# A 96-byte gap in front of one weight buffer, and 32 bytes behind it

## The reference, cut to what matters

```python
u = rms_norm(h, norm1_g)
p_rwkv, p_nsa = split(u @ w_in)                  # w_in: 1024 x 3096
y = concat(rwkv7_time_mix(p_rwkv), nsa_attention(p_nsa))
h = h + y @ w_out
h = h + (silu(rms_norm(h) @ w_gate) * (rms_norm(h) @ w_up)) @ w_down      # 1024 -> 2816 -> 1024
# then, in each of two layers: half a feed-forward, a mixer (even_w_in / odd_w_in), half a feed-forward
```

## Time and profile before

| | us |
|---|---|
| median of three runs | 1424.02 |
| lowest and highest run | 1423.72 and 1424.87 |
| span of the profiled execution | 1422.4 |
| TensorE busy in it | 1395.2 |
| VectorE busy | 944.7 |
| ScalarE busy | 691.0 |

### The profile page before, as it was taken

How to read it: one execution, slowest core, us unless ns; L and a number is a source line. 1 busy time by engine, 2 the same in 40 slices (tenths; PEclk the granted TensorE clock), 3 DMA queues, 4 the chain that set the end, 5 groups by cost and what they waited for, 6 DMA issues and landing times. The chain is left out here.

```text
span 1422.4 us, 25483 instructions
## 1 busy us (share of the span) xinstructions
PE 1395.2 (98%) x10044; PEld 1286.2 (90%) x10044; DVE 944.7 (66%) x1539; ACT 691.0 (49%) x1107; POOL 82.9 (6%) x137
## 2 busy tenths in 40 slices
PE   8999999999999999999999999999999999999997
PEld 8898888999989999899989999999998988899997
DVE  5778567766668666567577666676665676676665
ACT  6764545433454443376654433444433655643342
POOL 1030010000020000000000000100000123000000
PEclk9999999999999999999999999999999999999999
DMA  9344005645526555433356545365554423465540
GB/s 359 135 160 185 2 25 228 222 177 183 197 108 228 209 184 177 178 104 133 120 207 224 189 177 182 129 229 198 194 177 178 149 90 134 177 222 180 194 158 30
DMA packets 33069, 239.47 MB, mean 168 GB/s; under 512 B 6864, under 2 KB 13280, under 8 KB 14304
## 3 DMA queue, kind: packets, MB, share of 16 engines
q1 hardware_dynamic: 30320, 234.84, 45.6%
q10 hardware_dynamic: 2672, 3.58, 0.7%
HBM read 236.15 MB, written 2.25 MB: 168 GB/s over the span
## 5 line engine op out<-in xcount | busy, mean ns | idle before, releaser
L498 PE MATMUL ps<-uT_h,w_gu 128*128 128x256 f32 x3520 | 614.1, 279 | 2.5 <-ACT uT_h L1316 2.5
L498 PEld LDWEIGHTS ps<-uT_h,w_gu 128*128 128x128 f32 x3520 | 538.0, 188 | 13.8 <-issue 5.0
L498 PE MATMUL ps<-uT_l,w_gu 128*128 128x256 f32 x1760 | 478.8, 279 | 0.0
L498 PE MATMUL ps<-w_dn,h_r 128*128 128x512 f32 x1320 | 325.7, 396 | 0.3 <-DVE h_r L2070 0.3
L498 PEld LDWEIGHTS ps<-uT_l,w_gu 128*128 128x128 f32 x1760 | 325.5, 188 | 0.0
L498 PEld LDWEIGHTS ps<-w_dn,h_r 128*128 128x128 f32 x1320 | 239.6, 188 | 51.3 <-issue 1.4
L1368 ACT CAST w_gu<-ring 128x2048 fp32r<-128x2048 f32 x110 | 210.0, 1909 | 156.2 <-PE ps L498 155.6
L2028 DVE TENSOR_TENSOR w_gu<-ring,w_gu 128x2048 fp32r<-128x2048 f32 x110 | 252.1, 2292 | 35.2 <-ACT w_gu L1368 35.2
L2061 DVE TENSOR_TENSOR us<-ps,bc 128x256 f32<-128x256 f32 x110 | 46.5, 423 | 203.2 <-PE ps L498 203.2
L1381 ACT ACTIVATE wk<-wk 128x256 f32<-128x256 f32 x110 | 46.1, 419 | 260.7 <-DVE wk L2059 260.7
L1374 ACT CAST w_dn<-ring 128x1024 fp32r<-128x1024 f32 x110 | 115.7, 1052 | 82.8 <-PE ps L498 82.7
(11 more groups left out here) (398 smaller groups left out, 1696.0 us busy)
## 6 DMA issues: line engine op xcount, KB each, us to landing
ring<-wstream SPq DMA_DIRECT2D x144, 1536.0 KB, 6.6
cst<-consts_in SPq DMA_DIRECT2D x1, 2185.0 KB, 13.7
wk<-t_row ACTq DMA_DIRECT2D x1, 2048.0 KB, 8.0
wk<-masks_in SPq DMA_DIRECT2D x1, 1216.0 KB, 24.1
x<-x_in SPq DMA_DIRECT2D x2, 512.0 KB, 4.7
ring<-wstream SPq DMA_DIRECT2D x1, 1024.0 KB, 8.8
inh<-gains ACTq DMA_DIRECT2D x2, 512.0 KB, 9.6
tri_blocks<-wk SPq DMA_DIRECT2D x3, 256.0 KB, 2.8
```

The costliest lines, as they stand in the source:

```text
L498: return pe.matmul(o, l, r, start=start, stop=stop, skip_group_check=True)
```

## The change

Two unused allocations are made: 24 floats (96 bytes per partition) ahead of inh, and 8 floats (32 bytes) behind it. inh starts 96 bytes later, and every buffer behind it 128 bytes later. x, xn, uT and yT stay. Modulo 128, only inh has a new place: 96 past that of x, uT, yT and ring, which is the place that wk had and has. No instruction is added, removed or reordered.

```diff
         uT = sb("uT", [P, KC, T])
         yT = sb("yT", [P, KC, T])
+        sb("pad_in_front", [P, 24])
         inh = sb("inh", [P, KC * 3 * P])
+        sb("pad_behind", [P, 8])
         gb = inh[:, 0:2 * D].rearrange("p (a b) -> p a b", b=D)
         sb("gate_r", [P, 2 * KC * 24])
         ring = sb("ring", [P, RING, SLOT])
```

## The result

| | before | after |
|---|---|---|
| median, us | 1424.44 (four runs) | 1433.08 (four runs, 1432.88 to 1433.3) |
| span of the profiled execution | 1422.4 | 1431.5 |
| TensorE busy in it | 1395.2 | 1404.3 |

A forecast was written before the change was run, and what follows sets the result against it. TensorE, busy 98% of the span, was taken as the bound. Span 1422.4 less 0.95 us from w_in, all other terms 0, gave 1421.45, with 1.6 us around it 1423.1 us; range 1421.7 to 1425.2.

The forecast's parts named there:

- w_in's matmuls on in_h: In stage w_in, each step falls from 120.0 to 117.8 ns; over 576 matmuls 1.27 us.
- How much of it passes on: Of w_in's 192 triples, 144 (432 matmuls) pass their gain to the end: 0.95 us, bounds 0 to 1.96.
- 40 triples: Five w_in blocks between TensorE's stops at 19.09 and 38.47 us, claimed to pass their gain on.
- the 24 triples: First three of w_in's six blocks from 40.4 to 59 us, claimed to pass their gain on.
- Casts, low parts, later uses of inh: Cast into in_h, low part read from it, attention scores, exponentials, gains: taken as 0; casts and low parts bounded at 0.07 us.
- Everything behind inh moves by 128 bytes: Buffers behind inh keep their places modulo 128, so the cost was taken as 0.
- one number explains three stages: 3.4 ns saved per stationary load lying 96 bytes off fits w_in 120.0, even_in 117.8 and feed-forward 116.6 ns.
- The rival of the longer period: Period beyond 128 bytes, so 5280 gate and up matmuls change: 18 us slower (1442) or 5 us faster (1418.7); chance 0.06.
- the 1.6 us around the span: Time outside the profiled span, added to the forecast span of 1421.45 us to give 1423.1 us.
- The prediction's rival: The place has no price; w_in's 120.0 ns comes from something else in that stage; time 1424.0, chance 0.22.

The follow-up runs named there:

- e2: Against the kernel before the change: inh moved by 96 bytes, everything behind it by 256; 1424.21 us, ratio 1.0001.
- e1: Against the kernel before the change: inh stays, everything behind it moved by 128 bytes; 1433.59 us, ratio 1.0063.
- p1: TensorE alone, model left out: 60 matmuls of 256 columns (24 of 512) per operand distance, 0 to 480 bytes; steps 117.3 to 120.0 ns.
- e3: Against the kernel before the change: every buffer from x on, uT included, moved by 128 bytes; 1424.44 us, ratio 0.9999.
- p2: TensorE alone, model left out: feed-forward chunks in the kernel's order, three for each of 64 pairs of distances; last chunks 8213 to 8568 ns.
- e6: Against the kernel before the change: wk alone moved by 32 bytes, w_gu at distance 0 from the activations; 1435.85 us, ratio 1.0078.
- e10: Against the kernel before the change: w_gu, inh, gate_r and ring at 64 bytes from the activations modulo 256, ffb at 0; 1403.03 us, ratio 0.9859.
- e8: Against the kernel before the change: wk alone moved by 96 bytes, w_gu at distance 64 from the activations; 1413.3 us, ratio 0.9923.

## Why the prediction was wrong, step by step

*w_in's matmuls on in_h: 120.0 to 117.8 ns.* The number came true (117.8 in the four blocks, 118.1 over all of the stage), but in part by luck. Modulo 256 the change has in_h 96 and ring_r 128 bytes off the activations. With in_h alone off, as the forecast had it, the blocks stand at 118.5 (e2), with ring_r alone off at 119.1 (e1). So the 96 bytes bring 1.5 of the 2.2 ns, and the rest came with the 128 bytes that the forecast put at nothing.

*How much of it passes on: 0.95 us.* Right in kind, too large in size. After starts with a lag of 0.62 us, which is there at 11.4 us, ahead of the first weights (among the other kernels this offset goes from -0.33 to +1.51). The copy for which VectorE waits until 95.78 starts at 95.84 now: 0.62 - 0.06 = 0.56 us have passed on. The first two stretches give 0.25 us up to the stop at 38.84 (forecast 40 triples, 0.26); the stop at 56.46 takes back what the three blocks ahead of it had gained, so the 24 triples give nothing instead of 0.16; and the ten blocks behind it give 0.30, not 0.53, because outside the four blocks that I had measured the step fell by less than 2.2 ns. In e2 by the same reckoning 0.43 us pass on, in e1 0.20.

*Casts, low parts, later uses of inh: 0.* Right as far as it can be seen: in e2, where nothing else differs, the time is unchanged.

***Everything behind inh moves by 128 bytes. Places modulo 128 stay, so I take 0.*** This is the step that failed. e1 has this part alone and the whole loss; e2 has the other part alone and none; p1 has the period, 256 bytes. It was worth 9.3 us: 5280 x 1.82 - 2640 x 0.27 ns = 8.9 in the feed-forward layers, and some 0.4 for even_h's and odd_h's matmuls, which moved by the same 128 bytes (117.3 to 118.3 ns). Less w_in's 0.56 that makes 8.7, against 8.6 between the medians.

*The argument that one number explains three stages.* The trace held just two distances of all-stationary placement, 0 (w_in) and 224 (feed-forward), and a mixture of both. Any period that tells 0 from 224 fits them. "Modulo 128" was a choice, not a reading, and the diff's 96 + 32 = 128 made it look natural. even_in's 117.8 fitted by 0.1 ns, which I took for a confirmation. It was luck: e3 has the same distances, and there the same 94 steps go from 610.02 to 621.02 us, 117.0 ns each; and in e2 an arrangement with two thirds of the loads at 96 bytes stands at 118.5. Also p1's 117.3 at 96 bytes and 117.9 at 224 in one sequence, and 118.6 and 116.7 in another, show how little a match of 0.1 ns meant there.

*The rival of the longer period* had the mechanism, the place and the test right, and too small a chance, 0.06. Its price of up to 18 us took the worst known distance; 8.6 came. "Nothing speaks for it" was true, but nothing spoke against it either, and the trace could not have: this is an unknown with 5280 matmuls behind it, so each nanosecond is 5 us, either way. The sum's small slips decide nothing: the 1.6 us around the span came from the median of one set of runs and the span of another execution, where runs that have both show 1.8. A range that takes in the bounds of the unknown costs had to run from about 1418 to 1442.

Beside the rows stands the Trainium skill, page "SBUF — State Buffer", section "Who interferes with whom": TensorE never waits on anyone, with independent read ports for moving data and weights. As a rule on other engines it agrees with p2, where TensorE alone has the kernels' chunks within 2 ns. The prediction's rival read more into it, that a place has no price, and the measurement decides against that: p1 has steps from 117.3 to 120.0 ns by distance alone. Whether the two ports hinder each other, no run shows. The page "TensorE: Matmul & The Clock Gate", section "Back-to-back issue gap", gives the columns over 2.4 GHz plus 2.5 ns for a single matmul, apart from any stream of loads and matmuls. For 256 columns that makes 109.2 ns, an estimate by that page; the best pattern of this kernel's streams, 113.3, is 4 ns above it.

**What stays open**: why 256 bytes, and what in the memory or the array makes one distance cheap. A clash between the weight load and the moving data of a neighbouring matmul would fit all runs, but none measures it. Nor do the runs tell what decides which pattern a layer falls into.

## What to carry to other kernels

In a kernel bound by a stream of 128x128 loads with few columns, where two operands lie relative to each other in a partition is worth measuring by itself, in the sequence that the kernel really runs: here it is worth 2.3% between e6 and e10, for a few unused bytes. And a claim that a layout is unchanged "modulo n" is a claim on n: if the trace cannot show the period, the shift has to be priced with all matmuls that it touches, in both directions, however small its cause looks; or, when a buffer must move, both operands of the hot matmuls should move together, as in e3, or by a multiple of 256 bytes, as in e2.

## What was not expected of the hardware

- Places of the two operands count modulo 256 bytes: steps per 256 columns at distances 0, 32, ... 224 of 120.0, 118.3, 117.8, 117.3, 118.6, 120.0, 117.8 and 117.9 ns, and the same again from 256 on.
- The price depends on what ran ahead. Gate and up at distance 96 take 118.6 ns beside down's distance 32 and 117.3 beside 160 (p2), at distance 64 they take 117.8 or 113.9 over a chunk.
- One arrangement can hold two patterns, 8213 and 8420 ns a chunk (e8), and in e8's trace a whole layer of 22 chunks stays in the one in which it starts. In p2 the pair (64, 64) goes 8241, 8458, 8249 instead.
- A matmul of 512 columns takes 228.9 ns at distance 0 (227.0 at 256), one of the two worst places for those of 256, and 233.7 at 96, the best for them in p1. What is good for one shape is bad for the other.
